# A fused attention block on one core: first sums by K tile, and 29 visits instead of 31 in the input stage

## The chip, the cores and the metric

One core of a Trainium2 chip runs the whole program in one launch; nothing is shared with another core. The metric is the device time of one execution in microseconds (us), and less is better. Names of engines: TensorE (PE; PEld is its weight load), VectorE (DVE), ScalarE (ACT), GpSimd (POOL), SyncE (SP, which issues nearly all DMAs).

## What is computed

The reference is one decoder block with 256 tokens and a model width of 2048, all in float32:

```python
ada = c @ w_ada[l] + b_ada[l]
shift, scale, gate = jnp.split(ada, 3, axis=-1)
h = rms_norm(x, g_pre[l]) * (1.0 + scale[:, None]) + shift[:, None]

proj = h @ w_in[l]
(q_mla, c_kv, k_rope, q_diff, k_diff, v_diff,
 gate_mla, gate_diff, mg_mla, mg_diff) = jnp.split(proj, split_points, axis=-1)
...
y_mla = (o_mla * jax.nn.silu(gate_mla)) @ w_o_mla[l]
...
y_diff = (o_diff * jax.nn.silu(gate_diff)) @ w_o_diff[l]

merged = jax.nn.sigmoid(mg_mla) * y_mla + jax.nn.sigmoid(mg_diff) * y_diff
y = merged @ w_out[l]

x = x + gate[:, None] * rms_norm(y, g_post[l])
```

What this case turns on is its beginning: `h` depends on `c @ w_ada`, a product of one row with a matrix of 2048 x 6144, so h can't be finished before the columns of `w_ada` that belong to it are read.

## The kernel before

**Pieces.** Every weight matrix is read once, in pieces of 512 KB (256 rows of K by 512 columns in most jobs) into a ring of 4 slots, `w_raw`. A float32 product is made of three products of rounded halves. For each piece ACT rounds the weights (CAST, `w_hi`, line 1029), DVE takes what is left (`w_lo`, line 1558), and TensorE runs 12 matmuls of 512 columns: 4 of high h by high weight (line 1877), then 8 at line 1891. ACT may round piece p only when piece p - 4 is used and its DMA has landed.

**The input stage.** The first 70 pieces are worked off while h is still being made, in 8 periods. Period j has what is needed to use pair j of K tiles (256 rows of h), and at its end stands a turn: TensorE transposes the sums of `c * w_ada` for the next pair (`turn_ada`, line 1610), ACT adds them up (`sum_mod`, 987) and makes shift and gain (`make_mod`, 995 and 997), then the high part of h for the two K tiles (`make_h`, 1006) and the full h (`make_full`, 1018), and DVE takes the difference (`make_h_lo`, 1455), the low part of h. The sums themselves are made on DVE, two rows of `w_ada` at a time (1309), between its work on the pieces.

**The order.** It is written out by hand. The table `PERIODS` says which piece stands where: a number is a piece of one of the two q accumulators, which stay in PSUM; a tuple is a visit, one or more pieces of a job that owns PSUM banks only for the time of the visit. A visit's result is copied out by ACT (`act_early`, 756), or added on DVE (`add_early`, 1150), and a later visit of that job may be seeded, which is ACT copying the partial sum back into PSUM (`act_seed`, 766). Where those steps stand is counted in pieces: a copy stands two pieces behind the end of its visit, a sum one piece behind the turn, the high part of h two behind it, the full h and the low part three behind it (one less each for turn 1). On ACT, in each piece, the order is CAST, then the full h, then copies and seeds, then the high part of h, then the sum. All queues run strictly in that order.

**Who waits.** The first piece that uses a pair of K tiles waits for its high part of h before its first matmul, and for its low part before its last four; in such a piece (called opening below) the four matmuls with the low weight go first, for that reason. Before, pairs 1 to 7 are opened by pieces 10, 18, 26, 36, 45, 55 and 65, and the turns stand ahead of pieces 8, 15, 23, 31, 41, 51 and 61.

**The front.** Before piece 0, PE transposes x (line 1801), then adds up the sums of pair 0: two from `ada_acc`, made on DVE, and one straight from the last rows of `w_ada` (`first_sum`, 1617), then runs five matmuls whose result nobody reads (`keep_clock`, 1624). DVE makes shift and gain of both K tiles in one go (1434 to 1436), but stands at that time in the first half of `w_lo` of piece 0 (1553); ACT makes the high part of h (980), DVE the full h (1445) and the low part (1450).

Of the kernel before, what the change touches and what calls it, by code (L numbers as in the profile page):

```python
# [82 lines left out]
def make_jobs():  # L83
# [22 lines left out]
    [(("ckv", 0), (2, 3, 4)), 0, (("q", 2), (3, 4)), 1, TURN, (("gate", 1), (3, 4))],  # L106
    [(("gate", 3), (3, 4, 5)), 0, (("gate", 2), (3, 4, 5)), 1, TURN, (("vd", 0), (4, 5))],
    [(("vd", 1), (4, 5, 6)), 0, (("gate", 0), (4, 5, 6)), 1, TURN, (("q", 2), (5, 6))],
    [(("ckv", 0), (5, 6, 7)), 0, (("q", 2), (7,)), 1, (("gate", 0), (7,))],
# [3 lines left out]
SEEDED = [8, 9, 10, 12, 13, 14, 15, 16, 17, 19, 20, 21, 22, 23, 24]  # L113
# [16 lines left out]
def hybrid_block(nc, x, c, positions, w_ada, b_ada, g_pre, w_in, g_kv, w_ukv,  # L130
# [78 lines left out]
    with ExitStack() as ctx:  # L209
# [1184 lines left out]
        def _(eng):  # L1394
# [35 lines left out]
            def first_mod():  # L1430

                eng.wait_ge(ada_turned, 1)
                first_out = ps[:, 2, 0:4 * P:P]
                dve.tensor_tensor(mod_shift[:, 0:2], first_out[:, 0:2], cols[:, V_SHIFT:V_SHIFT + 2], ALU.add)
                link(eng, dve.tensor_tensor(mod_gain[:, 0:2], first_out[:, 2:4], cols[:, V_GPRE:V_GPRE + 2], ALU.mult))
                dve.tensor_tensor(mod_gain[:, 0:2], mod_gain[:, 0:2], cols[:, V_SCALE:V_SCALE + 2],
                                  ALU.add).then_inc(mod_first, 1)
# [105 lines left out]
            for p, (a, kind, n, i, first, last) in enumerate(pieces):  # L1543
                rows = gate_rows_on.get(p, [])
                for r in rows[:1]:
                    gate_row(r)(eng)
                if p not in POOL_LO:
                    eng.wait_ge(hi_done, p + 1)
                if kind == "kr":
                    dve.tensor_tensor(kr_half(p, 1), kr_raw_piece(p), kr_half(p, 0).bitcast(F32),  # L1550
                                      ALU.subtract).then_inc(lo_done, 1)
# [406 lines left out]
```

## Time and profile before

| | us |
|---|---|
| median of 3 runs | 766.87 |
| lowest, highest | 766.79, 767.28 |
| the profiled execution, its own time | 767.12 |
| its span, first to last instruction | 765.3 |
| PE busy in the span | 749.6 (98%) |
| DVE busy | 562.4 (73%) |
| ACT busy | 420.0 (55%) |

The profile is of one execution, which took 767.12 us; 1.8 us of them lie outside of the span. It is 0.25 us above the median of the runs. Starts in its timeline are in us from the start of the span. "PE busy" is the time in which a matmul is in flight, by modelled ends, so that a short delay between two matmuls shows in the distance of their starts and not as idle time.

### The profile page before, as it was taken

Reading aid. Unit: us, or ns where it says so; the run is one execution under the profiler, and the core shown is the slowest. Engines: PE = TensorE matmul, PEld = TensorE weight load, DVE = VectorE, ACT = ScalarE, POOL = GpSimd, SP = SyncE. Lnnn points to the kernel's source line nnn. Section 1 sums busy time; section 2 is a strip of 40 time slices with the busy share of each in tenths; the row PEclk is TensorE's granted clock in tenths of the full one; section 3 lists DMA queues with packets and bytes.
Section 4 is the critical chain, followed back from the end, with each engine's and each line's share of the span. In section 5 each row is a group of like instructions: output and inputs, shape, how many; then the busy total and the mean of one; then the engine's idle time right before and its main releaser. Section 6 shows DMA issues by size and latency. Waiting matters only on the chain.

```text
span 765.3 us, 10103 instructions
## 1 busy us (share of the span) xinstructions
PE 749.6 (98%) x3679; PEld 625.4 (82%) x3679; DVE 562.4 (73%) x824; ACT 420.0 (55%) x638; POOL 21.6 (3%) x94
## 2 busy tenths in 40 slices
PE   5999999999999999999999999999999999999997
PEld 5887788888888988888888888888888888888885
DVE  4899999889868579888887778676554556465554
ACT  4588777765567554544545565655444444444441
POOL 2000000000000000000000000011100000000000
PEclk9999999999999999999999999999999999999999
DMA  9999999998674789888886575655566656567642
GB/s 338 395 392 395 380 390 338 354 371 287 186 225 126 211 280 311 284 273 282 290 291 194 162 218 184 165 169 165 179 180 194 193 177 205 186 207 246 223 156 110
DMA packets 132556, 189.72 MB, mean 248 GB/s; under 512 B 10325, under 2 KB 68122, under 8 KB 132250
## 3 DMA queue, kind: packets, MB, share of 16 engines
q1 hardware_dynamic: 132240, 188.77, 75.5%
q8 instruction: 29, 0.48, 0.2%
q10 hardware_dynamic: 266, 0.30, 0.1%
q14 instruction: 21, 0.17, 0.1%
HBM read 185.90 MB, written 2.10 MB: 246 GB/s over the span
## 4 chain that ended last, share of the span: by engine, by line
PE 90%; ACT 2%; DVE 2%; DMA 2%; SPq 2%; issue 1%; DVEq 0%; POOLq 0%; POOL 0%; ACTq 0%
PE ps L1901 17%; PE ps L1903 17%; PE ps L1902 16%; PE ps L1891 13%; PE ps L1860 8%; PE ps L1877 7%; PE ps L1863 4%; DMA w_raw<-in_w_in 2%; SPq L525 2%; ACT w_both L1029 1%; PE ps L1698 1%; DVE ada_acc L1309 1%; PE ps L1683 1%; PE ps L1713 1%; DVE w_both L1558 1%
## 5 line engine op out<-in xcount | busy, mean ns | idle before, releaser
L1558 DVE TENSOR_TENSOR w_both<-w_raw,w_both 128x1024 fp32r<-128x1024 f32 x247 | 300.5, 1222 | 160.1 <-ACT w_both L1029 158.8
L1029 ACT CAST w_both<-w_raw 128x1024 fp32r<-128x1024 f32 x248 | 258.9, 1049 | 246.3 <-PE ps L1903 183.7
L1891 PE MATMUL ps<-w_both,h_both 128*128 128x512 f32 x560 | 138.8, 390 | 0.0
L1891 PEld LDWEIGHTS ps<-w_both,h_both 128*128 128x128 f32 x560 | 105.0, 188 | 22.8 <-DVE w_both L1558 0.7
L1901 PE MATMUL ps<-w_both,h_both 128*128 128x512 f32 x296 | 116.8, 395 | 0.0
L1903 PE MATMUL ps<-w_both,h_both 128*128 128x512 f32 x296 | 115.4, 390 | 0.0
L1902 PE MATMUL ps<-w_both,h_both 128*128 128x512 f32 x296 | 115.2, 389 | 0.0
L1877 PE MATMUL ps<-w_both,h_both 128*128 128x512 f32 x280 | 76.0, 393 | 0.9 <-ACT h_both L980 0.6
L1309 DVE SCALAR_TENSOR_TENSOR ada_acc<-ada_ring,cols,ada_acc 128x512 f32<-128x512 f32 x98 | 69.6, 745 | 0.5
L1901 PEld LDWEIGHTS ps<-w_both,h_both 128*128 128x128 f32 x296 | 55.6, 188 | 12.7 <-issue 1.7
L1903 PEld LDWEIGHTS ps<-w_both,h_both 128*128 128x128 f32 x296 | 55.5, 188 | 11.7
L1860 PE MATMUL ps<-h_both,w_both 128*128 128x512 f32 x256 | 64.9, 395 | 0.0
L1902 PEld LDWEIGHTS ps<-w_both,h_both 128*128 128x128 f32 x296 | 55.6, 188 | 11.0
L1877 PEld LDWEIGHTS ps<-w_both,h_both 128*128 128x128 f32 x280 | 51.6, 188 | 12.5 <-issue 2.0
L1860 PEld LDWEIGHTS ps<-h_both,w_both 128*128 128x128 f32 x256 | 46.1, 189 | 9.7 <-issue 1.3
L1901 PE MATMUL ps<-w_both,o_hi 128*128 128x512 f32 x128 | 50.2, 392 | 0.0
L1903 PE MATMUL ps<-w_both,o_lo 128*128 128x512 f32 x128 | 49.8, 389 | 0.0
L1902 PE MATMUL ps<-w_both,o_hi 128*128 128x512 f32 x128 | 49.8, 389 | 0.0
L1309 DVE SCALAR_TENSOR_TENSOR ada_acc<-gate_ring,cols,ada_acc 128x512 f32<-128x512 f32 x60 | 44.8, 747 | 2.5 <-DMA gate_ring<-in_w_ada 1.4
L1901 PE MATMUL ps<-w_both,m_hi 128*128 128x512 f32 x116 | 45.2, 390 | 0.0
L1903 PE MATMUL ps<-w_both,m_lo 128*128 128x512 f32 x116 | 45.2, 389 | 0.0
L1902 PE MATMUL ps<-w_both,m_hi 128*128 128x512 f32 x116 | 45.1, 389 | 0.0
(265 smaller groups left out, 847.1 us busy)
## 6 DMA issues: line engine op xcount, KB each, us to landing
w_raw<-in_w_in SPq DMA_DIRECT2D x177, 512.0 KB, 4.5
ada_ring<-in_w_ada SPq DMA_DIRECT2D x128, 256.0 KB, 6.4
gate_ring<-in_w_ada SPq DMA_DIRECT2D x32, 512.0 KB, 5.2
w_raw<-in_w_out SPq DMA_DIRECT2D x32, 512.0 KB, 3.7
w_raw<-in_w_o_mla SPq DMA_DIRECT2D x16, 512.0 KB, 4.0
w_raw<-in_w_o_diff SPq DMA_DIRECT2D x16, 512.0 KB, 4.0
w_raw<-in_w_ukv SPq DMA_DIRECT2D x16, 256.0 KB, 3.4
x_tok<-in_x SPq DMA_DIRECT2D x2, 1024.0 KB, 6.0
```

The costliest lines, as they stand in the source:

```text
L525: sp.dma_start(ada_slot(n)[:, :, s, :], w_ada[0, 2 * q * P:2 * (q + 1) * P, col:col + 2 * P] .rearrange("(t p) n -> p t n", p=P)).then_inc ...
L1029: act.copy(w_hi[:, p % RING, :], w_raw[:, p % RING, :]).then_inc(hi_done, 1)
L1309: ins = dve.scalar_tensor_tensor(out=acc, in0=src, scalar=cc, in1=acc, op0=ALU.mult, op1=ALU.add)
L1558: dve.tensor_tensor(w_lo[:, p % RING, :], w_raw[:, p % RING, :], w_hi[:, p % RING, :].bitcast(F32), ALU.subtract).then_inc(lo_done, 1)
L1683: mm(ps[:, 4 + w, lo:lo + keys], lhsT=qnT[:, 2 * u + w, t * P:(t + 1) * P], rhs=knT[:, 2 * u + w, 0:keys], start=t == 0, stop=False, skip_ ...
L1860: mm(ps[:, b0 + c, :], lhsT=w_hi[:, p % RING, (2 * r + c) * P:(2 * r + c + 1) * P], rhs=h_both[:, :, 4 * i + r, :], start=first and r == 0 ...
L1863: ins = mm(ps[:, b0 + c, 0:SEQ], lhsT=w_lo[:, p % RING, (2 * r + c) * P:(2 * r + c + 1) * P], rhs=h_hi[:, 4 * i + r, :], start=False, stop ...
L1877: mm(ps[:, b0 + t, :], lhsT=h_hi[:, 2 * i + r, t * P:(t + 1) * P], rhs=w_hi[:, p % RING, r * CH:(r + 1) * CH], start=fresh and r == 0, sto ...
L1891: ins = mm(ps[:, b0 + t, :], lhsT=side[:, 2 * i + r, t * P:(t + 1) * P], rhs=w[:, p % RING, r * CH:(r + 1) * CH], start=False, stop=last a ...
L1901: mm(o, lhsT=s_hi[:, k, q], rhs=hi, start=fresh and r == 0, stop=False, skip_group_check=kind == "early")
L1902: mm(o, lhsT=s_hi[:, k, q], rhs=lo, start=False, stop=False, skip_group_check=kind == "early")
L1903: ins = mm(o, lhsT=s_lo[:, k, q], rhs=hi, start=False, stop=last and r == tiles - 1, skip_group_check=kind == "early")
```

## The change

It has two halves. In the front, the sums of pair 0 are arranged by K tile: K tile 0 has PSUM bank 2, K tile 1 has bank 3, and a new semaphore `first_half` tells DVE when the first is complete; DVE makes shift and gain of each K tile by itself, before it touches `w_lo` of piece 0, which is now one instruction; the full h of pair 0 moves from DVE to ACT. Four matmuls of 512 columns on the identity, whose result nobody reads, come first on PE, and `keep_clock` has one matmul instead of five. In the visits of the first period, ACT copies a result out one piece sooner.

In the input stage the table has 29 visits instead of 31, and 6 instead of 8 of them are added on DVE. There are still 70 pieces, 7 turns and the same places of the sums behind a turn, but visits run over the period borders: the turns stand ahead of pieces 8, 15, 23, 32, 41, 51 and 62, and pairs 1 to 7 are opened by pieces 10, 17, 25, 34, 43, 53 and 64.

The core of the diff:

```diff
-    [(("ckv", 0), (0, 1)), 0, (("vd", 0), (1,)), (("vd", 1), (1,)), 1, TURN, (("gate", 3), (1,)), (("gate", 0), (1,))],
-    [(("gate", 1), (1, 2)), 0, (("gate", 2), (1, 2)), 1, TURN, (("q", 2), (1, 2))],
-    [(("vd", 0), (2, 3)), 0, (("vd", 1), (2, 3)), 1, TURN, (("gate", 0), (2, 3)), (("gate", 3), (2,))],
...
+    [(("ckv", 0), (0, 1)), 0, (("vd", 0), (1,)), (("vd", 1), (1,)), 1, TURN, (("gate", 3), (1,)), (("gate", 1), (1, 2))],
+    [0, (("gate", 2), (1, 2)), (("gate", 0), (1,)), 1, TURN, (("q", 2), (1, 2, 3))],
+    [0, (("vd", 0), (2, 3)), (("vd", 1), (2, 3)), 1, TURN, (("gate", 3), (2, 3, 4))],
...
         for v in COPIED:
-            act_after[visit_end[v] + 2].append(act_early(v))
+            act_after[visit_end[v] + (1 if visit_end[v] < turn_at[1] else 2)].append(act_early(v))
...
                 eng.wait_ge(xT_copied, KT // 2)
-                eng.wait_ge(mod_first, 1)
                 for k in range(2):
+                    eng.wait_ge(mod_first, k + 1)
                     act.activation(h_hi[:, k, :], xnT[:, k, :], ACT.Identity, scale=mod_gain[:, k:k + 1],
                                    bias=mod_shift[:, k:k + 1]).then_inc(h_first_hi, 1)
+                for k in range(2):
+                    act.activation(stage[:, 0, k * SEQ:(k + 1) * SEQ], xnT[:, k, :], ACT.Identity,
+                                   scale=mod_gain[:, k:k + 1], bias=mod_shift[:, k:k + 1]).then_inc(h_first_full, 1)
...
+            def first_mod(k):
+
+                if k == 0:
+                    eng.wait_ge(first_half, 1)
+                else:
+                    eng.wait_ge(ada_turned, 1)
+                dve.tensor_tensor(mod_shift[:, k:k + 1], ps[:, 2 + k, 0:1], cols[:, V_SHIFT + k:V_SHIFT + k + 1], ALU.add)
+                dve.scalar_tensor_tensor(out=mod_gain[:, k:k + 1], in0=ps[:, 2 + k, P:P + 1],
+                                         scalar=cols[:, V_GPRE + k:V_GPRE + k + 1],
+                                         in1=cols[:, V_SCALE + k:V_SCALE + k + 1], op0=ALU.mult,
+                                         op1=ALU.add).then_inc(mod_first, 1)
...
+                if p == 0:
+                    first_mod(0)
+                    first_mod(1)
...
-                    dve.tensor_tensor(w_lo[:, 0, 0:CH], w_raw[:, 0, 0:CH], w_hi[:, 0, 0:CH].bitcast(F32), ALU.subtract)
-                    first_mod()
...
+            def first_sum(src, cc, first, last=False):
+
+                for k in range(2):
+                    for part in range(2):
+                        ins = mm(ps[:, 2 + k, part * P:(part + 1) * P], lhsT=src(2 * part + k), rhs=cc,
+                                 start=first and part == 0, stop=False, skip_group_check=True)
+                    if last and k == 0:
+                        ins.then_inc(first_half, 1)
...
+            for i in range(4):
+                mm(ps[:, 6, :].rearrange("p (c n) -> p c n", c=4), lhsT=ident[:, :],
+                   rhs=ident[:, :].unsqueeze(1).to_broadcast([P, 4, P]), start=True, stop=True)
...
-            keep_clock(5)
+            keep_clock(1)
```

On DVE, in the front, from the last row of the first sums to the first low part of h. Before:

```order
L1426 SCALAR_TENSOR_TENSOR ada_acc<-ada_ring_96,cols,ada_acc 128x512 [waits ada_used,ada_in7]
L1553 TENSOR_TENSOR w_both<-w_raw,w_both 128x512 [waits hi_done]
L1434 TENSOR_TENSOR mod_shift<-ps,cols 128x2 [waits ada_turned]
L1435 TENSOR_TENSOR mod_gain<-ps,cols 128x2
L1436 TENSOR_TENSOR mod_gain<-mod_gain,cols 128x2 [waits dve_step]
L1555 TENSOR_TENSOR w_both<-w_raw,w_both 128x512
L1445 TENSOR_SCALAR stage<-xnT,mod_gain,mod_shift 128x256 [waits xT_copied,mod_first]
L1445 TENSOR_SCALAR stage<-xnT,mod_gain,mod_shift 128x256
L1450 TENSOR_TENSOR h_both<-stage,h_both 128x256 [waits h_first_hi,h_first_full] x2
```

And now:

```order
L1429 SCALAR_TENSOR_TENSOR ada_acc<-ada_ring_96,cols,ada_acc 128x512 [waits ada_used,ada_in7]
L1439 TENSOR_TENSOR mod_shift<-ps,cols 128x1 [waits first_half]
L1440 SCALAR_TENSOR_TENSOR mod_gain<-ps,cols 128x1
L1439 TENSOR_TENSOR mod_shift<-ps,cols 128x1 [waits ada_turned]
L1440 SCALAR_TENSOR_TENSOR mod_gain<-ps,cols 128x1
L1557 TENSOR_TENSOR w_both<-w_raw,w_both 128x1024 [waits hi_done]
L1451 TENSOR_TENSOR h_both<-stage,h_both 128x256 [waits h_first_hi,h_first_full] x2
```

The gains of both K tiles moved ahead of `w_lo`, and the two instructions that made the full h left DVE.

On TensorE behind turn 2, the third and fourth piece (the rows of the first two, pieces 15 and 16, are left out; each begins at line 1877). Before:

```order
L1877 MATMUL ps<-w_both,h_both 128x512 [waits hi_done,early_seeded,ada_read]
L1877 MATMUL ps<-w_both,h_both 128x512 x3
L1891 MATMUL ps<-w_both,h_both 128x512 x4
L1891 MATMUL ps<-w_both,h_both 128x512 [waits lo_done]
L1891 MATMUL ps<-w_both,h_both 128x512 x3
L1877 MATMUL ps<-w_both,h_both 128x512 [waits h_hi_ready,hi_done]
L1877 MATMUL ps<-w_both,h_both 128x512 x3
```

And now, where line 1883 is what was 1877, and 1897 what was 1891:

```order
L1883 MATMUL ps<-w_both,h_both 128x512 [waits h_hi_ready,hi_done]
L1883 MATMUL ps<-w_both,h_both 128x512 x3
L1897 MATMUL ps<-w_both,h_both 128x512 [waits lo_done]
L1897 MATMUL ps<-w_both,h_both 128x512 x3
L1897 MATMUL ps<-w_both,h_both 128x512 [waits h_lo_ready]
L1897 MATMUL ps<-w_both,h_both 128x512 x3
L1883 MATMUL ps<-w_both,h_both 128x512 [waits hi_done]
```

The wait for the high part of h (`h_hi_ready`) stood in the fourth piece behind the turn and stands in the third, piece 17.

On ACT behind turn 2, the rows from the sum to the full h are the same before and now but for line numbers. Now:

```order
L990 ACTIVATE sum_junk,mod_sums<-ps 128x128 [waits ada_turned]
...
L1000 ACTIVATE mod_gain<-mod_sums,cols 128x1
L1032 CAST w_both<-w_raw 128x1024 [waits piece_used,raw_in1]
L756 COPY gate_part_sum<-ps 128x1024 [waits piece_used]
L766 COPY ps<-gate_part_sum 128x1024 [waits early_copied,ada_read]
L1009 ACTIVATE h_both<-xnT,mod_shift,mod_gain 128x256 [waits mod_ready]
L1009 ACTIVATE h_both<-xnT,mod_shift,mod_gain 128x256
L1032 CAST w_both<-w_raw 128x1024 [waits piece_used,raw_in2]
L1021 ACTIVATE stage<-xnT,mod_shift,mod_gain 128x256 [waits h_lo_ready]
```

Between the gains and the high part of h stand a CAST, the copy of visit 10 and the seed of visit 12, as before; nothing moved here, only the piece that waits for it on TensorE.

## Rows read from the trace of the kernel before

**Rows 1.** The page, part 1: busy time, share and instructions of each engine

```profile
PE 749.6 (98%) x3679; PEld 625.4 (82%) x3679; DVE 562.4 (73%) x824; ACT 420.0 (55%) x638; POOL 21.6 (3%) x94
```

**Rows 2.** Busy time by stretch: us, PE, PEld, DVE, ACT, POOL, then granted clock, DMA share, GB/s

```profile
28.00:50.00 22.00, 22.00 (x101) 18.21 (x100) 20.92 (x27) 14.64 (x27) 0.00 (x0) 1.00 1.07 393
```

**Rows 3.** Timeline, TensorE: two pieces in a row, the first turn, then piece 10

```profile
29.44 1.07 PE L1877 MATMUL ps<-w_both,h_both 128*128 128x512 f32 x4
...
32.16 1.07 PE L1877 MATMUL ps<-w_both,h_both 128*128 128x512 f32 x4
...
45.77 0.60 PE L1610 MATMUL ps<-ident,ada_acc 128*128 128x128 f32 x4
...
51.68 1.08 PE L1877 MATMUL ps<-w_both,h_both 128*128 128x512 f32 x4
...
54.75 1.08 PE L1877 MATMUL ps<-w_both,h_both 128*128 128x512 f32 x4
```

**Rows 4.** Timeline, all engines, the front: sums, first gains, first product

```profile
1.16 0.29 POOL L610 TENSOR_SCALAR_AFFINE_SELECT ident<-ident 128x128 f32<-128x128 f32 x1 [0.24 <-POOL ident L608]
...
8.43 0.35 PE L1792 MATMUL ps<-ident,vec_rows 69*128 69x69 f32 x1 [8.43 <-DMA vec_rows<-in_g_subln]
...
13.03 7.56 DVE L1426 SCALAR_TENSOR_TENSOR ada_acc<-ada_ring,cols,ada_acc 128x512 f32<-128x512 f32 x11
...
21.08 1.05 PE L1617 MATMUL ps<-ones,ada_acc 128*128 128x128 f32 x8
...
22.00 0.69 DVE L1553 TENSOR_TENSOR w_both<-w_raw,w_both 128x512 fp32r<-128x512 f32 x1 [1.42 <-ACT w_both L1029]
...
22.61 0.15 DVE L1434 TENSOR_TENSOR mod_shift<-ps,cols 128x2 f32<-128x2 f32 x1
...
23.12 1.09 ACT L980 ACTIVATE h_both<-xnT,mod_shift,mod_gain 128x256 fp32r<-128x256 f32 x2 [1.15 <-DVE mod_gain L1436]
...
23.87 1.17 PE L1877 MATMUL ps<-w_both,h_both 128*128 128x512 f32 x4 [0.62 <-ACT h_both L980]
...
30.02 1.05 ACT L1029 CAST w_both<-w_raw 128x1024 fp32r<-128x1024 f32 x1 [1.82 <-DMA w_raw<-in_w_in]
```

**Rows 5.** Transposes of x on TensorE, early and late stretch (ns min/median/max)

```profile
L1801 PE MATMUL ps<-x_diag,x_tok x9: 421/421/551, 9.7 to 11.5; 128*128 128x128 f32 x9
...
L1801 PE MATMUL ps<-x_diag,x_tok x12: 275/275/275, 15.9 to 17.2; 128*128 128x128 f32 x12
```

**Rows 6.** Timeline, around turn 2: turn, rounding of piece 16, h of pair 2

```profile
65.65 0.60 PE L1610 MATMUL ps<-ident,ada_acc 128*128 128x128 f32 x4
...
65.86 1.05 ACT L1029 CAST w_both<-w_raw 128x1024 fp32r<-128x1024 f32 x1 [0.43 <-DMA w_raw<-in_w_in]
...
71.85 1.09 ACT L1006 ACTIVATE h_both<-xnT,mod_shift,mod_gain 128x256 fp32r<-128x256 f32 x2
...
75.05 0.68 DVE L1455 TENSOR_TENSOR h_both<-stage,h_both 128x512 fp32r<-128x512 f32 x1
```

**Rows 7.** Timeline, turns 3, 5, 6 and 7, and the low part of h behind each

```profile
89.12 0.66 PE L1610 MATMUL ps<-ident,ada_acc 128*128 128x128 f32 x4
...
97.02 0.68 DVE L1455 TENSOR_TENSOR h_both<-stage,h_both 128x512 fp32r<-128x512 f32 x1
...
139.33 0.60 PE L1610 MATMUL ps<-ident,ada_acc 128*128 128x128 f32 x4
...
147.18 0.69 DVE L1455 TENSOR_TENSOR h_both<-stage,h_both 128x512 fp32r<-128x512 f32 x1
...
167.01 0.60 PE L1610 MATMUL ps<-ident,ada_acc 128*128 128x128 f32 x4
...
174.43 0.68 DVE L1455 TENSOR_TENSOR h_both<-stage,h_both 128x512 fp32r<-128x512 f32 x1
...
194.70 0.60 PE L1610 MATMUL ps<-ident,ada_acc 128*128 128x128 f32 x4
...
201.91 0.68 DVE L1455 TENSOR_TENSOR h_both<-stage,h_both 128x512 fp32r<-128x512 f32 x1
```

More of the change, by code:

```diff
@@ L102 @@
      (("gate", 2), (0,)), (("gate", 3), (0,)), 1, TURN, (("q", 2), (0,))],
-    [(("ckv", 0), (0, 1)), 0, (("vd", 0), (1,)), (("vd", 1), (1,)), 1, TURN, (("gate", 3), (1,)), (("gate", 0), (1,))],
-    [(("gate", 1), (1, 2)), 0, (("gate", 2), (1, 2)), 1, TURN, (("q", 2), (1, 2))],
-    [(("vd", 0), (2, 3)), 0, (("vd", 1), (2, 3)), 1, TURN, (("gate", 0), (2, 3)), (("gate", 3), (2,))],
[L106 to L109, printed above, removed]
+    [(("ckv", 0), (0, 1)), 0, (("vd", 0), (1,)), (("vd", 1), (1,)), 1, TURN, (("gate", 3), (1,)), (("gate", 1), (1, 2))],
+    [0, (("gate", 2), (1, 2)), (("gate", 0), (1,)), 1, TURN, (("q", 2), (1, 2, 3))],
+    [0, (("vd", 0), (2, 3)), (("vd", 1), (2, 3)), 1, TURN, (("gate", 3), (2, 3, 4))],
+    [0, (("ckv", 0), (2, 3, 4)), (("gate", 0), (2,)), 1, TURN, (("gate", 2), (3, 4, 5))],
+    [0, (("gate", 1), (3, 4)), (("gate", 0), (3, 4, 5)), 1, TURN, (("vd", 0), (4, 5, 6))],
+    [0, (("vd", 1), (4, 5, 6)), (("q", 2), (4, 5, 6)), 1, TURN, (("ckv", 0), (5, 6, 7))],
+    [0, (("q", 2), (7,)), 1, (("gate", 0), (6, 7))],
 ]
@@ L112 @@
 OPENING = [v for v, visit in enumerate(VISITS) if visit[1] not in [w[1] for w in VISITS[:v]]]
-SEEDED = [8, 9, 10, 12, 13, 14, 15, 16, 17, 19, 20, 21, 22, 23, 24]
+SEEDED = [v for v in range(8, 24) if v != 11]
 ADDING = [v for v in range(len(VISITS)) if v not in OPENING and v not in SEEDED]
@@ L1428, in first_rows @@
                     ins.then_inc(done, amount)
[L1430 to L1437, printed above, removed]
+            def first_mod(k):
[8 more added lines that the diff above has]
+                                         op1=ALU.add).then_inc(mod_first, 1)
             def make_first_h_lo():
-                eng.wait_ge(mod_first, 1)
-                eng.wait_ge(xT_copied, KT // 2)
                 full = [stage[:, 0, k * SEQ:(k + 1) * SEQ] for k in range(2)]
-                for k in range(2):
-                    dve.tensor_scalar(full[k], xnT[:, k, :], mod_gain[:, k:k + 1], mod_shift[:, k:k + 1], ALU.mult,
-                                      ALU.add).then_inc(h_first_full, 1)
                 for k in range(2):
@@ L1612, in turn_ada @@
                 ins.then_inc(ada_turned, 1)
-            def first_sum(src, cc, first):
-                for b in range(4):
-                    ins = mm(ps[:, 2, b * P:(b + 1) * P], lhsT=src(b), rhs=cc, start=first and b == 0, stop=False,
-                             skip_group_check=True)
+            def first_sum(src, cc, first, last=False):
[5 more added lines that the diff above has]
+                        ins.then_inc(first_half, 1)
                 return ins
@@ L1623, in keep_clock @@
                 for i in range(count):
-                    mm(ps[:, 3, 0:P], lhsT=x_tok[:, 0, 0:P], rhs=x_diag[:, 0, :], start=True, stop=True)
+                    mm(ps[:, 1, 0:P], lhsT=x_tok[:, 0, 0:P], rhs=x_diag[:, 0, :], start=True, stop=True)
             def first_direct(q):
@@ L1633, in first_direct, with first_acc @@
                 ins.then_inc(ada_direct, 1)
-            def first_acc(t, done, first=False):
+            def first_acc(t, done, first=False, last=False):
                 pe.wait_ge(done, KT // 2)
-                return first_sum(lambda b: ada_acc[:, t, b * P:(b + 1) * P], ones[:, :], first)
+                return first_sum(lambda b: ada_acc[:, t, b * P:(b + 1) * P], ones[:, :], first, last)
             def group(g):
@@ L1806, in _ @@
             first_direct(7)
-            first_acc(0, ada_used).then_inc(ada_turned, 1)
-            keep_clock(5)
+            first_acc(0, ada_used, last=True).then_inc(ada_turned, 1)
+            keep_clock(1)
             for p, (a, kind, n, i, first, last) in enumerate(pieces[:NP - LAST_GROUP]):
```

6 lines of the change are left out of this document (2 added, 4 removed).

## The prediction

> **What bounds the kernel now.** I read the page's busy times first: TensorE is busy for 749.6 of 765.3 us [rows 1], so only three things can move the time: when PE starts its row of pieces, what holds it up between them, and how much work it has. The last doesn't change: 70 pieces before and after, 7 turns, and four unread matmuls come in front where four others go. The windows show that in the input stage DVE is nearly as full as PE (20.92 of 22 us) and the DMA engines are full, with a share of 1.07 at 393 GB/s [rows 2]. So in its first third the stage has three engines that run at one pace, and a gain of one of them is soon lost to another.
>
> The timeline of PE gives the unit: 29.44 to 32.16, so one piece takes 2.72 us [rows 3]. Turn 1 starts at 45.77 and piece 10, the third behind it, at 51.68, which is turn + 5.91 (two pieces of 2.72 and 0.47 for the turn and its restart). Piece 10 opens pair 1 and takes until 54.75, 3.07 instead of 2.72: 0.35 lost. So the kernel before already has one border where pair j is opened two pieces behind the turn, and it costs 0.35. Its other borders leave three pieces (pairs 2 and 3) or more. The change makes the distance two pieces at all seven.
>
> **Front.** PE's last sums start at 21.08; DVE is then in half of `w_lo` from 22.00 and makes the gains only at 22.61; ACT's high part of h starts at 23.12 and the first product at 23.87 [rows 4]. Now bank 2 is complete after half of the sums, 21.08 + 0.53 = about 21.6, seen on DVE at 21.7 (my reading of the 1.05 us row). Two instructions of 0.15 make it 22.0, ACT is free from its CAST of piece 0 at 21.98, and the high part starts at 22.1 instead of 23.12: the first product starts 1.0 us sooner, at 22.85. What was `w_lo` of piece 0 comes at 22.45 and takes 1.22, so it ends at 23.7, just when the low weight is wanted (22.85 + 0.13 + 0.91 = 23.9). The full h on ACT costs another 1.09, as its high part does, so ACT's CAST of piece 1 comes when it came before (22.1 + 2.2 = 24.3; before, 23.12 + 1.09 = 24.2). DVE is rid of 0.73 us of work.
>
> The gain is then eaten. ACT's CAST of piece 3 starts at 30.02 after 1.82 us of waiting for its DMA [rows 4], and ends at 31.07. PE, which took piece 3 at 32.16, can take it from about 31.25: 0.9 is left. The queue of DMAs is full, so the landings don't come sooner. The sooner copies fit into the waits of ACT for DMAs and cost nothing; what they cover is PE's wait for a free bank, which the trace doesn't show as a wait at all. At turn 2 nothing is left of the gain, and this is the point: the CAST of piece 16 starts at 65.86, behind a DMA (0.43 of waiting) [rows 6], and the sum of turn 2 stands behind it on ACT. The chain to h of pair 2 starts from a landing, whether PE comes to turn 2 at 65.65 or at 65.2.
>
> **Warm-up matmuls.** The transposes of x show 421 ns a record at 9.7 to 11.5 us and 275 ns from 15.9 on; nine starts in 1.8 us are 0.22 each, twelve in 1.3 are 0.12 [rows 5]. That is the lower and the upper clock level (1.2 and 2.4 GHz), although the page's row of granted clock shows 1.00 throughout. The four new matmuls start with the identity (1.16 + 0.29) and have 8 records of four times the columns: 3.8 us at the upper, 7.2 at the lower level, so they end between 5.3 and 8.7, and the first real one starts at 8.43 [rows 4]. Cost: at most 0.2, in a stretch that has slack. Gain: the transposes end at about 17.2 instead of 19.3, but the sums wait for DVE, whose eleven rows run from 13.03 to 20.59 [rows 4]. So nothing on the path. The Trainium skill, "TensorE: Matmul & The Clock Gate", Part 1, says that the slow level is the default and activity releases it, so that such matmuls would be worth having where the transposes set the end; here they don't, and the sum is the same by either.
>
> **The borders**, now one by one. I take the time at which h was ready in the trace of before, since ACT's order behind a turn is the same, and set it against the new place at which PE wants it: the high part at turn + 5.91 less 0.2 for the load of weights (the first product started 0.2 behind the end of its h), the low part after 4 + 4 more matmuls, at turn + 5.91 + 1.81 = turn + 7.72. A hold-up adds a restart of 0.13, as behind a turn.
>
> Pair 2: the high part ends at 71.85 + 1.09 = 72.94, the low part at 75.05 + 0.68 = 75.73 [rows 6]; on ACT the copy and the seed of 1.0 each stand between the gains and h. Piece 17 would start at 71.5 and starts at 73.1; its last four matmuls would start at 75.1 and start at 75.8. It ends at 75.8 + 0.91 + 0.13 = 76.85. Five more pieces (13.6) give turn 3 at 90.45, where it was at 89.12 [rows 7]: **+1.3**. The small hold-ups between turns 2 and 3 before are in that: 23.47 us for eight pieces that take 22.2.
>
> Pair 3: the low part ends at 97.70, turn + 8.58 [rows 7]. Wanted at turn + 7.72: 0.86 + 0.09 for the semaphore + 0.13 = **1.1**. The high part, three ACT instructions of 1.0 sooner than the low part, is wanted 1.8 sooner and is within it. Pair 5: low part at 147.87, turn + 8.54: **1.05**. Pair 4: in the plan of before nothing stood between gains and h there; now the seed of visit 18 does, so it is like pairs 3 and 5: **1.1**. Pair 6: 175.11, turn + 8.10, no seed: **0.6**. Pair 7: 202.59, turn + 7.89: **0.4**. Sum of pairs 3 to 7: 4.25. Before, from turn 3 to turn 5 PE lost 0.3 (50.21 us for 18 pieces and two turns, which take 49.9 [rows 7]) and nothing between turns 5 and 6 (27.68 for ten pieces); 0.2 of it may go. Two visits fewer save ACT and DVE a copy and an addition here and there, for which nobody waits at these places.
>
> Behind the last border PE has no idle time that an earlier or later start could fill: what it arrives with goes to the end. Sum: 1.3 + 4.25 - 0.2 = **+5.3 us**. Against the profiled execution, 767.1 + 5.3 = 772.4; its own time is 0.25 above the median of the runs, so the median should be 766.9 + 5.3 = **772.2**.
>
> Bounds of what the trace doesn't show: the low part at the borders may come sooner where DVE is less full (down to the end of the full h plus 0.8, which for pairs 3 to 5 saves nothing, since there CAST and `w_lo` stand ahead of it; for pairs 6 and 7 it takes both to 0.1): -0.8. A copy that waits for a late piece may stand ahead of the sum: +1.0 at one or two borders.
>
> **Rivals.** (a) *h comes sooner than I read it, and the borders are covered.* If ACT came to the chain of each pair 1 to 2 us sooner, because fewer visits leave it free, the front's 1.0 and the 1.2 between turns 2 and 3 would be kept: 766.9 - 2.2 = 764.7. Against it: ACT waits for the turn itself at turns 3 to 7 and the rest is instructions in a row. It decides where the two parts are there by turn + 5.7 and turn + 7.6; pair 1, at the same distance and with no seed in its chain, lost only the 0.35. Chance 0.08. (b) *Only the high part costs.* If the low part is in time everywhere, pair 2 costs 1.6 + 0.13 less 1.2, and the rest next to nothing: 767.5. For it speaks that pair 1 lost little at the same distance. Chance 0.06. (c) *The clock falls.* PE is idle from about 17.2 to 19.2, where it was busy, and `keep_clock` is shorter. If PE's clock fell to the lower level, the 24 records of the sums would take 0.1 more each, 2.5 us, and the first pieces too; the slack of 1.6 to 1.9 us ahead of piece 17 takes most: 773 to 775. The same page of the Trainium skill says that the clock falls back after idle time, so by it this is the danger of the front's change; no row of before shows such a fall behind a break of 2 us. Chance 0.06. (d) *The delays feed on each other*, a copy or seed ahead of h waiting for a piece that came late, one more ACT instruction of 1.0 at each of four borders: 776. Chance 0.05. The forecast, 770 to 774: 0.75.
>
> **Numbers.** Predicted 772.2. The range reaches from 769.6 (pairs 6 and 7 free, and half of pairs 3 to 5) to 774.2 (two borders with one more instruction, or the clock), which leaves out (a), (b) and most of (d). A measurement of this kernel can tell about 0.2% (1.5 us) from no change. Slower by more: forecast, (c), (d), 0.87; within: most of (b), 0.05; faster: (a), 0.08.
>
> **What would show it.** In the profile after: the first product at 22.9; piece 3 directly behind its CAST at 31.2; on PE a gap in piece 17 of some 2.5 us whose releasers are ACT's high part and DVE's low part; turn 3 near 90.4; in pieces 25, 34 and 43 about 1 us ahead of the last four matmuls, released by `make_h_lo`; less in 53 and 64; from there on everything 5.3 us later than before. It is wrong if those pieces take 2.72, or if the sum of turn 2 starts well ahead of 66.8.

## The result

| | before | after |
|---|---|---|
| median | 767.21 us (6 runs) | 772.81 us (6 runs) |
| lowest, highest | 766.79, 767.44 | 772.34, 773.00 |
| ratio, 95% interval | | 1.0072 [1.0062, 1.0083] |
| profiled execution, its own time | 767.12 | 772.92 |
| its span | 765.3 | 771.1 |

The change makes the kernel slower, by 5.6 us between the medians. Predicted were 772.2 us, in a range of 769.6 to 774.2. Two executions of the experiments below, one of ten of the front alone (1081.69 us) and one of four with the break filled (2697.82 us), were slow ones; they move the medians given by 0.03 us at most, and nothing is read from them.

The page of the kernel after, part 1:

```profile
PE 756.3 (98%) x3679; PEld 625.7 (81%) x3679; DVE 560.1 (73%) x820; ACT 421.4 (55%) x640; POOL 21.1 (3%) x94
```

PE has as many instructions as in [rows 1] and is busy for 6.7 us more. The largest part stands at the very start, where PE did nothing before: the four unread matmuls are in flight for 6.1 us, from which a shorter `keep_clock` and a break of 2.15 us (below) take off some 3.

```profile
1.51 6.10 PE L1794 MATMUL ps<-ident 128*128 128x512 f32 x8 [1.51 <-POOL ident L610]
```

The rest is the sums of pair 0 at a lower clock (below), and matmuls that are recorded as in flight while they wait: the table alone, which has neither the unread matmuls nor the lower clock, is busy for 750.9 us. So PE has no more work in the input stage, and the starts have to be read.

**The front** didn't come as forecast in this execution. The timeline, with the last releaser of each wait in brackets, then two windows (busy time by stretch: us, PE, PEld, DVE, ACT, POOL, granted clock, DMA share, GB/s):

```profile
19.31 1.39 PE L1617 MATMUL ps<-ones,ada_acc 128*128 128x128 f32 x8 [2.15 <-DVE ada_acc L1429]
...
20.48 1.92 PE L1617 MATMUL ps<-cols,ada_ring 128*128 128x128 f32 x8
...
23.67 1.14 ACT L980 ACTIVATE h_both<-xnT,mod_shift,mod_gain 128x256 fp32r<-128x256 f32 x2 [1.57 <-DVE mod_gain L1440]
...
24.41 0.95 PE L1883 MATMUL ps<-w_both,h_both 128*128 128x512 f32 x3 [0.34 <-ACT h_both L980]
```

```profile
16.00:20.00 4.00, 1.85 (x17) 1.68 (x16) 3.90 (x7) 1.17 (x2) 0.00 (x0) 1.00 1.08 392
20.00:24.00 4.00, 4.00 (x22) 3.88 (x21) 1.07 (x5) 1.37 (x2) 0.00 (x0) 0.57 1.08 393
```

PE waited 2.15 us for DVE ahead of the sums, and from 20 to 24 us its granted clock is 0.57: the lower of the two levels (1.2 GHz) for most of that stretch. Eight matmuls of 128 columns take 1.92 us, where eight took 1.05 [rows 4]. The first product starts at 24.41, 0.54 later than before and not 1.0 sooner.

**Behind turn 2**, all engines; `h_both` by ACT L1009 is the high part of h, by DVE L1456 the low part; L1883 are a piece's first four matmuls, L1897 its other eight, L1609 is the turn:

```profile
72.14 1.09 ACT L1009 ACTIVATE h_both<-xnT,mod_shift,mod_gain 128x256 fp32r<-128x256 f32 x2
...
73.37 1.17 PE L1883 MATMUL ps<-w_both,h_both 128*128 128x512 f32 x4 [0.82 <-ACT h_both L1009]
...
75.34 0.68 DVE L1456 TENSOR_TENSOR h_both<-stage,h_both 128x512 fp32r<-128x512 f32 x1
...
76.08 1.20 PE L1897 MATMUL ps<-w_both,h_both 128*128 128x512 f32 x4 [0.63 <-DVE h_both L1456]
...
90.73 0.60 PE L1609 MATMUL ps<-ident,ada_acc 128*128 128x128 f32 x4
```

These answer to [rows 6] and the first of [rows 7]: h is there at nearly the same time as before (72.14 for 71.85, 75.34 for 75.05), but now PE stands waiting for both parts. Piece 16 lasts 0.98 us more than 2.72, piece 17 another 1.02, and turn 3 comes at 90.73 instead of 89.12.

**Behind the later turns** only the low part is late. PE's waits summed up by what was waited for (total us, times, longest), from 15 to 225 us:

```profile
PEld ps L1897 <- DVE h_both L1456: 5.3, 6, 1.1
```

Then two of the six in the timeline, behind turns 3 and 6:

```profile
98.56 0.68 DVE L1456 TENSOR_TENSOR h_both<-stage,h_both 128x512 fp32r<-128x512 f32 x1
...
99.30 1.20 PE L1897 MATMUL ps<-w_both,h_both 128*128 128x512 f32 x4 [0.62 <-DVE h_both L1456]
...
171.31 0.60 PE L1609 MATMUL ps<-ident,ada_acc 128*128 128x128 f32 x4
...
178.73 0.68 DVE L1456 TENSOR_TENSOR h_both<-stage,h_both 128x512 fp32r<-128x512 f32 x1
...
179.47 1.20 PE L1897 MATMUL ps<-w_both,h_both 128*128 128x512 f32 x4 [0.25 <-DVE h_both L1456]
```

The low part starts 7.83 us behind turn 3 (7.90 before, [rows 7]) and 7.42 behind turn 6 (7.42 before). DVE and ACT did nothing slower. What changed is when PE asks. Only at pair 4 did the chain itself grow, as forecast: with a seed now ahead of h, its low part starts 7.83 us behind turn 4, where it started 7.43 behind it before.

**Behind the input stage** one more wait stands that before had nowhere. PE's waits from 225 to 300 us, then the place in the timeline (L1164 adds the last part of a gate to its sum, L1907 are pieces of the jobs that follow), and last the same addition in the kernel before (L1161):

```profile
PEld ps L1907 <- DVE gate_part_sum L1164: 0.6, 1, 0.6
```

```profile
249.65 1.21 DVE L1164 TENSOR_TENSOR gate_part_sum<-gate_part_sum,ps 128x1024 f32<-128x1024 f32 x1
...
250.92 0.19 PEld L1907 LDWEIGHTS ps<-w_both,h_both 128*128 128x128 f32 x1 [0.57 <-DVE gate_part_sum L1164]
```

```profile
245.46 1.22 DVE L1161 TENSOR_TENSOR gate_part_sum<-gate_part_sum,ps 128x1024 f32<-128x1024 f32 x1
```

It is the addition of gate 2. In the kernel before, that gate's last piece begins on PE at 242.42, and the addition starts 3.0 us later; now the piece begins at 243.37 and the addition starts 6.3 us later.

The whole difference of the two profiled executions, by distances of starts on PE beyond those of undisturbed pieces (2.72 us each):

| place | us |
|---|---|
| up to turn 3 (90.73 - 89.12) | +1.61 |
| pieces 25, 34, 43, 53, 64, which open pairs 3 to 7 | +0.98, +0.96, +1.00, +0.54, +0.28 |
| piece 61 | +0.16 |
| pieces 33 and 34 of before, held up no more | -0.22 |
| the addition of a gate, at 250.9 | +0.45 |
| sum | +5.8 (771.1 - 765.3) |

### The profile page after: what moved, and what is told of

The parts are those of the page before. It is cut to its first block, busy times and chain, and to the rows that moved or that the text cites. A ratio compares the mean times of both kernels' runs of the same rounds, so it can differ in the third digit from the quotient of the medians.

```text
span 771.1 us, 10096 instructions
## 1 busy us (share of the span) xinstructions
PE 756.3 (98%) x3679; PEld 625.7 (81%) x3679; DVE 560.1 (73%) x820; ACT 421.4 (55%) x640; POOL 21.1 (3%) x94
## 4 chain that ended last, share of the span: by engine, by line
PE 87%; DVE 5%; ACT 3%; issue 2%; DMA 2%; SPq 0%; DVEq 0%; POOLq 0%; POOL 0%; ACTq 0%
PE ps L1907 16%; PE ps L1909 16%; PE ps L1908 16%; PE ps L1897 12%; PE ps L1866 8%; PE ps L1883 6%; PE ps L1869 4%; DVE w_both L1557 1%; ACT w_both L1032 1%; DMA ada_ring<-in_w_ada 1%; DMA w_raw<-in_w_in 1%; PE ps L1700 1%; PE ps L1685 1%; PE ps L1715 1%; DVE ada_acc L1429 1%
## 5 line engine op out<-in xcount | busy, mean ns | idle before, releaser
L1897 PE MATMUL ps<-w_both,h_both 128*128 128x512 f32 x560 | 140.4, 391 | 2.8 <-DVE h_both L1456 2.8
L1897 PEld LDWEIGHTS ps<-w_both,h_both 128*128 128x128 f32 x560 | 104.5, 188 | 27.6 <-DVE h_both L1456 5.3
L1907 PE MATMUL ps<-w_both,h_both 128*128 128x512 f32 x296 | 117.0, 395 | 0.1
L1883 PE MATMUL ps<-w_both,h_both 128*128 128x512 f32 x280 | 76.0, 393 | 1.2 <-ACT h_both L1009 0.8
L1907 PEld LDWEIGHTS ps<-w_both,h_both 128*128 128x128 f32 x296 | 55.6, 188 | 13.2 <-issue 1.7
L1883 PEld LDWEIGHTS ps<-w_both,h_both 128*128 128x128 f32 x280 | 51.5, 188 | 12.6 <-issue 2.3
L1907 PE MATMUL ps<-w_both,o_hi 128*128 128x512 f32 x128 | 50.2, 392 | 0.0
L1907 PE MATMUL ps<-w_both,m_hi 128*128 128x512 f32 x116 | 45.2, 390 | 0.0
```

The source lines that it names most:

```text
L1883: mm(ps[:, b0 + t, :], lhsT=h_hi[:, 2 * i + r, t * P:(t + 1) * P], rhs=w_hi[:, p % RING, r * CH:(r + 1) * CH], start=fresh and r == 0, sto ...
L1897: ins = mm(ps[:, b0 + t, :], lhsT=side[:, 2 * i + r, t * P:(t + 1) * P], rhs=w[:, p % RING, r * CH:(r + 1) * CH], start=False, stop=last a ...
L1907: mm(o, lhsT=s_hi[:, k, q], rhs=hi, start=fresh and r == 0, stop=False, skip_group_check=kind == "early")
```

## The experiments

The **theory** going in: the table of visits costs everything, at the borders, by parts of h that come when they came before but are wanted one piece sooner; the front's gain is absorbed at the landing of piece 16. **Rivals:** the front costs time by the clock; only the high part of h costs; the delays come from something else in the new table, such as its seeds and copies.

### The table alone, and the front alone

`e1_plan_only` is the kernel before with the new table and the old front; `e2_front_only` is the kernel after with the old table.

```diff
-    [(("gate", 1), (1, 2)), 0, (("gate", 2), (1, 2)), 1, TURN, (("q", 2), (1, 2))],
+    [0, (("gate", 2), (1, 2)), (("gate", 0), (1,)), 1, TURN, (("q", 2), (1, 2, 3))],
...
-SEEDED = [8, 9, 10, 12, 13, 14, 15, 16, 17, 19, 20, 21, 22, 23, 24]
+SEEDED = [v for v in range(8, 24) if v != 11]
```

> The kernel before with the new table of 29 visits, and its old front. Theory (the borders cost, the front's gain or loss is absorbed ahead of the piece that opens pair 2): 5.3 us slower than before, piece 17 to 18 and the opening pieces 25, 34 and 43 some 1 us longer each, turn 3 at about 90.5. Rival (the front and its clock cost part of it): clearly less than the changed kernel's 5.6, say 4.5 to 5.0, and turn 3 sooner than the 90.7 of the changed kernel.

> The changed front with the old table of 31 visits. Theory: within 0.5 us of before, whether the first product starts at 24.4 or at 22.9, because the sum of turn 2 waits for the CAST of piece 16, which waits for a DMA that lands at about 65.9. Rival (the front is worth what it moves the first product by): 1.0 us faster where the clock stays up, 0.5 slower where it falls.

Measured: the table alone 772.71 us, ratio to the kernel before 1.0073 [1.0058, 1.0088]; the front alone 767.21, ratio 0.9998 [0.9988, 1.0008]. TensorE with the table alone, behind turn 2:

```profile
73.14 1.17 PE L1877 MATMUL ps<-w_both,h_both 128*128 128x512 f32 x4 [1.41 <-ACT h_both L1006]
...
75.85 1.20 PE L1891 MATMUL ps<-w_both,h_both 128*128 128x512 f32 x4 [0.62 <-DVE h_both L1455]
...
90.50 0.60 PE L1610 MATMUL ps<-ident,ada_acc 128*128 128x128 f32 x4
```

Here turn 2 came at 65.63, and the sum up to turn 3 is 90.50 - 89.12 = 1.38. The openings of pairs 3 to 7 lose 0.97, 0.98, 0.97, 0.59 and 0.27. So the table alone has the whole loss, and the front none of it.

The front alone shows what it does when the clock holds (first a window, then the timeline; the profiled execution took 767.02 us):

```profile
20.00:24.00 4.00, 3.51 (x26) 3.13 (x26) 2.57 (x7) 2.97 (x5) 0.00 (x0) 1.00 1.08 393
```

```profile
22.82 1.17 PE L1883 MATMUL ps<-w_both,h_both 128*128 128x512 f32 x4 [0.49 <-ACT h_both L980]
...
31.23 1.09 PE L1883 MATMUL ps<-w_both,h_both 128*128 128x512 f32 x4
...
65.45 0.63 PE L1609 MATMUL ps<-ident,ada_acc 128*128 128x128 f32 x4
65.74 1.05 ACT L1032 CAST w_both<-w_raw 128x1024 fp32r<-128x1024 f32 x1 [0.43 <-DMA w_raw<-in_w_in]
...
89.01 0.66 PE L1609 MATMUL ps<-ident,ada_acc 128*128 128x128 f32 x4 [0.17 <-DVE ada_acc L1312]
```

The first product is at 22.82 (forecast 22.85) and piece 3 at 31.23 (31.25). Of the 1.05 us gained, 0.93 is left at piece 3, 0.7 at turn 1 (45.06 for 45.77), 0.2 at turn 2 and 0.1 at turn 3, where DVE's sums hold the turn up. The rounding of piece 16 waits 0.43 for its DMA, the same as in [rows 6]: the landing sets the pace there, not the front.

### Which part of h holds PE up

`e3_h_first`: on ACT, in the piece in which both stand, the high part of h goes ahead of the copy and the seed.

```diff
+                if p in h_after:
+                    make_h(h_after[p])
                 for work in act_after[p]:
                     work(eng)
-                if p in h_after:
-                    make_h(h_after[p])
```

> The changed kernel with one thing moved: in a piece that has the high part of h and a copy or seed, ACT makes h first. Theory (the chain turn, sum, gains, CAST, copy, seed, h is what TensorE waits for): pair 2 gets h 2.0 us sooner, pairs 3, 4 and 5 1.0 sooner each, so the total falls by 4 to 5 us against the changed kernel, to 768 to 769; pairs 6 and 7, which have nothing to pass, keep their 0.5 and 0.3. Rival (what makes the borders dear is DVE, which is full when the low part is wanted, or the number of visits): less than 1.5 us back.

Measured: 773.51 us (772.87 to 774.48), ratio 1.0086 [1.0069, 1.0103]. The expectation missed by 5 us: nothing came back. The timeline behind turn 2:

```profile
69.95 1.09 ACT L1009 ACTIVATE h_both<-xnT,mod_shift,mod_gain 128x256 fp32r<-128x256 f32 x2
...
71.60 1.07 PE L1883 MATMUL ps<-w_both,h_both 128*128 128x512 f32 x4
...
75.14 0.68 DVE L1456 TENSOR_TENSOR h_both<-stage,h_both 128x512 fp32r<-128x512 f32 x1
...
75.88 1.20 PE L1897 MATMUL ps<-w_both,h_both 128*128 128x512 f32 x4 [2.30 <-DVE h_both L1456]
```

The high part came 2.2 us sooner, and piece 17 started on time, at 71.60. But the low part still stood at 75.14, since CAST and the full h come one piece later on ACT whatever stands behind the first CAST, and the whole delay (2.60 us over 2.72) fell in one wait ahead of the last four matmuls. That is the disproof of the rival by which only the high part costs: with the high part free, the low part alone has the full price.

### The clock in the front

`e4_fill_gap`: eight more unread matmuls in PE's break ahead of the sums.

```diff
             pe.wait_ge(xT_copied, 4)
+            keep_clock(8)
             first_acc(1, ada_odd, True)
```

> The changed kernel with eight more unread matmuls between the transposes of x and the first sums, where TensorE is idle for 2 us. Theory: granted clock 1.00 in the stretch from 20 to 24 us (it was 0.57 in the changed kernel's profile), first product at 22.9 instead of 24.4, and no change of the total by more than 0.4 us, because the wait at piece 17 takes it. Rival (the clock's fall goes through to the end): 1 to 1.5 us faster than the changed kernel.

Measured: 772.83 us, ratio 1.0072 [1.0055, 1.0088]. The total is that of the kernel after, as the theory has it. Its other half missed: the first product came at 23.94, not at 22.9.

```profile
8.00:12.00 4.00, 2.50 (x13) 2.42 (x14) 2.00 (x7) 2.43 (x3) 2.04 (x6) 0.75 1.04 353
...
20.00:24.00 4.00, 3.51 (x32) 3.35 (x31) 1.69 (x6) 1.85 (x3) 0.00 (x0) 1.00 1.07 387
```

```profile
23.94 1.17 PE L1884 MATMUL ps<-w_both,h_both 128*128 128x512 f32 x4 [0.49 <-ACT h_both L980]
```

With the break filled the clock is 1.00 from 20 to 24, but in this execution it was already 0.75 from 8 to 12, while the early matmuls and the transposes ran. The transposes ended late, the extra matmuls started only at 18.60, and the sums stood behind them until 20.38, where without them they start at about 19.2. That is why the first product is late, at full clock:

```profile
18.60 1.95 PE L1626 MATMUL ps<-x_diag,x_tok 128*128 128x128 f32 x16
20.38 1.06 PE L1617 MATMUL ps<-ones,ada_acc 128*128 128x128 f32 x8
```

So this run doesn't isolate the fall. The run before it comes nearer, by luck: in the profile of e3 the clock was 0.69 from 8 to 12 as well, the transposes ran on until 18.6 and left PE a wait of only 0.62 us, the clock was 1.00 from 20 to 24, and the first product came at 22.87. What e4 adds is how little the start counts behind turn 2: with the new table and ACT's order as it was up to there, first products at 22.65 (f3, below), 23.91 (e1), 23.94 (here) and 24.41 (after) give turn 3 at 90.10, 90.50, 90.57 and 90.73. Of 1.76 us at the start 0.63 are left at turn 3.

### Making the chain to h longer, and shorter

If the low part sets the price, a longer chain ahead of it must cost what it adds, as far as DVE isn't still busy with its own work, and a chain one piece shorter must give back the whole wait. `f3_full_twice` is the kernel after, where ACT makes the full h twice for pairs 3 to 7 (the first result is not used):

```diff
-                for b in range(2):
+                for c, b in ((1, 0), (1, 1), (0, 0), (0, 1)) if j >= 3 else ((0, 0), (0, 1)):
```

> The changed kernel with one cause doubled: for pairs 3 to 7 ACT makes the full h twice (once into an unused place), 0.98 us more ahead of the low part, and nothing else. Theory: the low parts come later by 0.86 at pairs 3, 4 and 5, where ACT's chain ends behind DVE's w_lo, and by 0.4 and 0.55 at pairs 6 and 7, where DVE's w_lo covers part of it, and each delay goes through: 3.5 us slower than the changed kernel, 776.3. Rival (openings wait for something that a longer chain hides behind, such as PSUM banks or w_lo): under 1 us slower.

Measured: 776.06 us (775.84, 776.28), ratio 1.0117 [1.0098, 1.0135]. Behind turn 3:

```profile
96.67 2.07 ACT L1021 ACTIVATE stage<-xnT,mod_shift,mod_gain 128x256 f32<-128x256 f32 x4
...
98.77 0.69 DVE L1456 TENSOR_TENSOR h_both<-stage,h_both 128x512 fp32r<-128x512 f32 x1 [0.75 <-ACT stage L1021]
...
99.52 1.20 PE L1897 MATMUL ps<-w_both,h_both 128*128 128x512 f32 x4 [1.47 <-DVE h_both L1456]
```

The openings of pairs 3 to 7 lose 1.80, 1.85, 1.82, 0.89 and 0.90: 0.82, 0.89, 0.82, 0.35 and 0.62 more than in the kernel after, 3.5 us in all for five more pairs of ACT instructions of 1.0 us each pair (2.07 for four instructions in the row). At pairs 6 and 7, 0.4 and 0.55 were expected. The theory's 776.3 was met.

`f1_h_chain_sooner`: gains and high part directly behind the sum, and the full h and the low part one piece sooner.

```diff
-        full_after = {place + 2: j for place, j in sum_after.items()}
+        full_after = {place + 1: j for place, j in sum_after.items()}
...
-                if p in h_after:
-                    make_h(h_after[p])
...
                     sum_mod(sum_after[p])
-                    if sum_after[p] > 1:
-                        make_mod(sum_after[p])
+                    make_mod(sum_after[p])
+                    make_h(sum_after[p])
```

> The changed kernel with the whole of the h chain one piece sooner: ACT makes the high part right behind the gains, in the piece of the sum, and the full h behind the next CAST, ahead of copies and seeds; DVE makes the low part one piece sooner. Theory (of the two parts, the low part is what opening pieces wait for, and its chain on ACT is too long by one CAST and the copies): low part at turn + 6.7 instead of + 7.9 to 8.6, wanted at + 7.7, so the openings of pairs 2 to 7 cost nothing, turn 3 comes near 89.0 (DVE's row of sums sets it), and the total falls by 5 to 6 us against the changed kernel, to 766.8 to 767.6. Rival (the plan of 29 visits is dear for another reason, banks or DVE): no more than 2 us back.

Measured: 769.30 us (769.11 to 771.06), ratio 1.0036 [1.0024, 1.0049]; the profile is of an execution of 770.83 us, in which the clock fell in the front. No piece waits for h at pairs 2 to 7 now, as the theory says (the low part of pair 3 starts 6.15 us behind the turn instead of 7.83), and pieces 25, 34, 43, 53 and 64 take 2.72 us each. Piece 17 is followed 0.25 us late, because the copy and the seed now stand ahead of the rounding of piece 18. But 2 us more than expected stayed, and they stand behind turn 1:

```profile
49.53 1.09 ACT L1009 ACTIVATE h_both<-xnT,mod_shift,mod_gain 128x256 fp32r<-128x256 f32 x2
50.53 1.03 ACT L1032 CAST w_both<-w_raw 128x1024 fp32r<-128x1024 f32 x1
...
51.70 1.17 PE L1879 MATMUL ps<-w_both,h_both 128*128 128x512 f32 x4 [1.70 <-ACT w_both L1032]
```

Pair 1 has its sum in the first piece behind its turn. There h now stands ahead of the rounding of piece 9, so PE waits 1.70 us for a weight instead of for h.

`f2_old_plan_h_sooner` is the same edit on `e2_front_only`, the old table.

> The old table of 31 visits with the changed front, and the same sooner h chain. Theory: only pair 1 had a short distance there, so piece 10 gives back 0.3, which turn 3 does not pass on, since DVE's sums are ready only at 88.9: within 0.4 us of before, like the changed front alone. Rival (DVE or ACT gain by the new order also between turns 2 and 3): 0.5 to 1.2 us faster than before.

Measured: 774.57 us (772.51 to 775.86), ratio 1.0103 [1.0087, 1.0118], a miss by 7 us to the wrong side. Behind turn 2, line 766 being the seed and L1879 a piece's first matmuls:

```profile
73.79 1.02 ACT L766 COPY ps<-gate_part_sum 128x1024 f32<-128x1024 f32 x1
74.87 0.76 PEld L1879 LDWEIGHTS ps<-w_both,h_both 128*128 128x128 f32 x4 [2.25 <-issue]
74.90 1.16 PE L1879 MATMUL ps<-w_both,h_both 128*128 128x512 f32 x4 [1.86 <-issue]
```

In the old table the piece three behind the turn wants a seed, not h. With the chain ahead of it, the seed ends at 74.81 and the piece starts then: piece 16 loses 2.01 us, pieces 24 and 42 1.00 each, and piece 8 1.98, as in f1. The profile is of the fastest of the four executions (772.51 us); what the others lost beyond it isn't in any trace. ACT's order and the table fit each other: the table before leaves room for a late h and needs an early seed.

### The best mixture

`g1_h_sooner_from_pair_2` leaves pair 1 as it was and makes f1's edit for pairs 2 to 7. `g2_pool` also moves the `w_lo` of two pieces, 13 and 22, from DVE to GpSimd, to relieve DVE ahead of turns 2 and 3.

```diff
-        full_after = {place + 1: j for place, j in sum_after.items()}
+        full_after = {place + (1 if j > 1 else 2): j for place, j in sum_after.items()}
...
-POOL_PART = [()] * 8
+POOL_PART = [(), (4,), (4,), (), (), (), (), ()]
```

> The changed kernel with the sooner h chain for pairs 2 to 7 only; pair 1 keeps its order (high part behind the CAST of piece 9, full h behind that of piece 10), since in the run with all pairs moved piece 9 waited 2.0 us for its CAST. Theory: the openings of pairs 2 to 7 cost nothing, the 2.0 at piece 9 are gone, turn 3 at 89.0 to 89.5, set by DVE's sums; the total 0 to 0.5 us above the kernel before, 767.0 to 767.5, so the plan's whole loss is the place of the h chain. Rival (the plan of 29 visits also loses elsewhere): 1.5 us or more above before.

> The same with w_lo of two pieces (13 and 22) made on GpSimd instead of DVE. Theory: between turns 1 and 3 DVE is the engine that sets the pace, so turn 3 comes up to 1.2 us sooner than without, 88.0 to 88.5, and the total 0.5 to 1.2 below it, under the kernel before. Rival (GpSimd is too slow or slows DVE): the pieces wait, and the total is 1 us or more above the other.

Measured: g1 768.30 us (767.97 to 768.58, 11 runs), ratio 1.0015 [1.0006, 1.0023]: 4.5 of the 5.6 us are back, and the new table is still behind the old by some 1.1, between the forecast (at most 0.5) and the rival (1.5 or more). Of PE's waits in g1, those at the turns (from 15 to 225 us) and the one for a gate's addition (from 225 to 300):

```profile
PEld ps L1610 <- DVE ada_acc L1313: 1.8, 3, 0.8
```

```profile
PEld ps L1908 <- DVE gate_part_sum L1165: 0.6, 1, 0.6
```

The waits for h are gone; piece 18 comes 0.84 us late for its rounding, behind a copy and a seed. The rest is turn 3 at 89.43 (+0.3), piece 61 that loses 0.47 ahead of turn 7, less the 0.22 saved, and the 0.45 of the gate's addition: 1.0 in sum. The turns now wait for DVE's sums of `c * w_ada`, the next limit.

g2 measured 769.80 us (769.15 to 770.58), ratio 1.0037 [1.0025, 1.0049], slower than g1; the rival expectation was right. L1313 are the sums of `c * w_ada`, two of them in its line:

```profile
58.84 2.40 POOL L647 TENSOR_TENSOR w_both<-w_raw,w_both 128x1024 fp32r<-128x1024 f32 x1 [46.45 <-ACT w_both L1032]
...
83.99 2.80 POOL L647 TENSOR_TENSOR w_both<-w_raw,w_both 128x1024 fp32r<-128x1024 f32 x1 [22.74 <-ACT w_both L1032]
84.43 3.57 DVE L1313 SCALAR_TENSOR_TENSOR ada_acc<-ada_ring,cols,ada_acc 128x512 f32<-128x512 f32 x2
...
90.45 0.66 PE L1610 MATMUL ps<-ident,ada_acc 128*128 128x128 f32 x4 [1.66 <-DVE ada_acc L1313]
```

The same subtraction takes DVE 1.22 us. What costs is less GpSimd's own 2.40 and 2.80 us (PE waits for them 0.2 us in all) than what DVE does meanwhile. One sum of L1313 takes it 0.75 us everywhere else in the input stage; the two that started while GpSimd was at its subtraction, at 58.96 and 84.43, took 2.83 and 2.90 us and ended 0.55 us behind its end. So each piece taken from DVE saved it 1.22 us and cost it 2.1, and the turns, which wait for DVE's sums, come later: behind pieces 14 and 22 they are 0.77 and 1.81 us late. No version of the new table was found that beats the kernel before.

## Why the prediction was right, step by step

- **No work is added, so only starts count.** Right: 3679 instructions on PE in both.
- **The front gains 1.0 us at the first product, and it is eaten by turn 2.** Right where the clock held (22.82 in the front alone, 0.2 of the gain left at turn 2, 767.21 in all). In the profiled execution of the kernel after the clock fell, as rival (c) has it, and the first product was 1.6 us later than that. The price that (c) put on it, up to 2.8 us on the total, was wrong for this kernel: its execution with the fall (mean granted clock 0.995) took 772.92, the five without (0.999) 772.34 to 773.00. Most of it went in the slack ahead of piece 17, as the same sentence of the rival allowed.
- **The break and the clock.** The prediction said that by the Trainium skill, "TensorE: Matmul & The Clock Gate", Part 1, idle time is the danger of the front's change, and that no row of before shows a fall behind a break of 2 us. A row of after does (0.57 from 20 to 24 us, behind a wait of 2.15), so the trace agrees with the page that it can happen. The trace adds that it need not: the front alone kept 1.00 in the same stretch, behind a wait of 2.03. The page says there of the warm-up that it differs from one execution to the next; here the fall seems to do so too, since one execution of six of the kernel after has a mean granted clock of 0.995 and the others have 0.999.
- **Pair 2 costs 1.3.** 1.38 with the table alone (90.50), 1.61 with the fall of the clock. Piece 17 was forecast at 73.1 and came at 73.14 and 73.37; its last four matmuls at 75.8, and came at 75.85 and 76.08.
- **Pairs 3 to 7 cost 1.1, 1.1, 1.05, 0.6, 0.4.** They cost 0.98, 0.96, 1.00, 0.54, 0.28: 3.76 for 4.25. Each term is 0.05 to 0.14 too large, because DVE came to the low part at up to 0.07 sooner behind the turn, and the wait for its result was smaller than the 0.09 put on it (99.30 is 0.74 behind 98.56, not 0.77). Rival (b), only the high part, falls with e3.
- **0.2 of the old hold-ups may go.** 0.22 went.
- **Behind the last border everything is 5.3 us later and stays so.** 5.35 at the end of the input stage (225.00 for 219.65), but not from there on. The step "nobody waits at these places" for the moved additions was wrong at one: between the last piece of gate 2 and the addition of its result, DVE now has a `w_lo`, six short instructions on the rotated key and another `w_lo`, and PE waits 0.6 us for the addition at 250.9, 0.45 of which is net. In the kernel before, the short instructions were done before that piece ended. It is there in e1, too, so it is the table's. Likewise piece 61 lost 0.16 that no term had. So 0.9 us came on top of the sum (0.3 at turn 3, 0.16 and 0.45) and 0.5 of its terms for pairs 3 to 7 didn't come: that the difference of the medians fits to 0.3 us (5.6 for 5.3) is in part luck. The other 0.3 of the 0.6 between 772.2 and 772.81 is the kernel before itself, 767.21 here where the prediction had 766.87.

That gate 2's addition is late *because* of its place in the new table is argued from the two timelines; no run moved it by itself. Whether turns one piece sooner, with DVE's sums ready for them, would make the table pay was not tried.

## What to carry to other kernels

When a plan moves a consumer forward in its queue and leaves the chain that feeds it in place, read where the chain's last instruction stands relative to its trigger in the old trace (here it starts 7.90, 7.85 and 7.42 us behind the turn) and subtract the consumer's new distance: the answer was good to 0.15 us at each of five borders. Where two parts of an operand are late in turn, as at pair 2, taking the first away gave nothing; it is the last one whose chain must be shortened, and in queues that run in order this moves something else back (a weight's rounding in f1, a seed in f2). Time gained ahead of a stretch in which the DMA engines are full can be worth nothing behind it: here 0.1 of 1.05 us was left at turn 3.

## What the runs showed of the hardware

- **A fall of the clock behind a break of some 2 us came in some executions and not in others.** Six profiles with the new front have PE waiting for 1.76 to 2.15 us ahead of the sums. Its granted clock from 20 to 24 us was 0.57 in that of after and 0.63 in that of f1, and 1.00 in those of the front alone, f3, g1 and g2. (In the other three, e3, e4 and f2, the clock was 0.69 to 0.75 from 8 to 12 us, the transposes ran on until 18.6 or later, and the sums had 1.00.) The fall is worth 1.6 us at the first product (24.41 for 22.82).
- **What it does to the total depends on the slack behind it.** In the kernel after it did nothing that the totals show. In f1 the profiled execution, which has the fall, took 770.83 us, and another with the same mean clock of 0.996 took 771.06; those with 0.999 to 1.0 took 769.11 to 769.30, some 1.8 less. Only the first was profiled, and a mean doesn't say where the clock was low. The traces suggest a reason: in the kernel after, pieces 16 and 17 lose 2.0 us to waits for h, which a late start only shortens; in f1 0.25 us behind piece 17 and 0.58 ahead of turn 3 are left. No run tested it.
- **GpSimd took 2.40 and 2.80 us for a subtraction of 128 x 1024 float32 values that takes DVE 1.22, and DVE was held up meanwhile.** The DVE instructions of 0.75 us that started during it took 2.83 and 2.90 us (g2).
